# Four weight units of three narrow stages take x before its norm, and the norm's scale is put on their results

## The reference, cut to what matters

```python
h = x * rsqrt(mean(x * x) + eps) * gain + shift      # gain and shift: one number for each of 1024 channels
u = h @ w_in
```

## Time and profile before

| what | value |
|---|---|
| median of three runs | 2800.35 us (2799.84 to 2803.69) |
| the profiled execution, its own time | 2799.17 us |
| its span, first to last instruction | 2797.3 us |
| mean granted clock of TensorE | 0.994 of full speed |
| TensorE busy | 98% of the span |
| VectorE, ScalarE, GpSimd busy | 74%, 44%, 19% |

### The profile page before, as it was taken

One profiled execution on the slowest core, in us unless ns is written; L12 is line 12 of the kernel. 1 busy time (PEld: TensorE's weight loads), 2 busy tenths in 40 slices (PEclk: granted clock), 3 DMA queues, 4 the chain that ended last, 5 costly groups with the idle time before them and its releaser, 6 DMA issues.

```text
span 2797.3 us, 40204 instructions
## 1 busy us (share of the span) xinstructions
PE 2732.1 (98%) x15618; PEld 2320.2 (83%) x15618; DVE 2067.0 (74%) x3773; ACT 1216.9 (44%) x2228; POOL 522.2 (19%) x449
## 2 busy tenths in 40 slices
PE   7999999999999999999988999999999999999998
PEld 5888878668888878888885999889999888888887
DVE  6989895568989896564766766765896677777776
ACT  5323233453232342222445545565556444444444
POOL 1111114300111101010050000345898000000000
PEclk9999999999999999999999999999999999999999
DMA  7555533223555445354441566424654556655554
GB/s 290 194 186 192 185 136 112 76 103 123 202 182 190 175 154 189 122 191 145 146 148 45 191 216 216 146 84 151 197 152 121 185 190 192 192 193 190 190 190 132
DMA packets 123261, 462.50 MB, mean 165 GB/s; under 512 B 13504, under 2 KB 26688, under 8 KB 109888
## 3 DMA queue, kind: packets, MB, share of 16 engines
q1 hardware_dynamic: 109248, 359.27, 39.5%
q0 software_dynamic: 13824, 100.67, 9.3%
HBM read 452.93 MB, written 6.95 MB: 164 GB/s over the span
## 4 chain that ended last, share of the span: by engine, by line
PE 90%; DVE 7%; issue 1%; ACT 1%; DMA 1%; POOL 1%; POOLq 0%; DVEq 0%; ACTq 0%
PE bank L283 28%; PE bank L284 27%; PE bank L285 27%; PE bank L2469 2%; DVE weight_lo L182 1%; DVE extension_ffn L920 1%; DVE nmax L1397 1%; DMA extension_ffn<-in_w_mods 1%; DVE arena L544 1%; PE bank L940 1%; PE bank L941 1%; PE bank L385 0%; PE bank L508 0%; DVE extension_mixer L1390 0%; POOL weight_lo L235 0%
## 5 line engine op out<-in xcount | busy, mean ns | idle before, releaser
L175 ACT ACTIVATE weight_hi<-weight_ring 128x512 fp32r<-128x512 f32 x1272 | 798.7, 631 | 1188.2 <-PE bank L285 1187.1
L182 DVE TENSOR_TENSOR weight_lo<-weight_ring,weight_hi 128x512 fp32r<-128x512 f32 x1110 | 839.4, 760 | 430.6 <-ACT weight_hi L175 428.9
L283 PE MATMUL bank<-operand_hi,weight_hi 128*128 128x256 f32 (+1 forms) x3168 | 1045.4, 330 | 16.8 <-DVE operand_lo L561 5.6
L284 PE MATMUL bank<-operand_lo,weight_hi 128*128 128x256 f32 (+1 forms) x3168 | 1032.8, 326 | 0.0
L285 PE MATMUL bank<-operand_hi,weight_lo 128*128 128x256 f32 (+1 forms) x3168 | 1032.6, 326 | 0.0
L283 PEld LDWEIGHTS bank<-operand_hi,weight_hi 128*128 128x128 f32 x3168 | 602.2, 190 | 86.1 <-issue 16.1
L284 PEld LDWEIGHTS bank<-operand_lo,weight_hi 128*128 128x128 f32 x3168 | 602.6, 190 | 53.1 <-issue 0.5
L285 PEld LDWEIGHTS bank<-operand_hi,weight_lo 128*128 128x128 f32 x3168 | 602.1, 190 | 50.4
L920 DVE SCALAR_TENSOR_TENSOR extension_ffn<-extension_ffn,silu_c 128x512 f32<-128x512 f32 x532 | 388.4, 779 | 1.7
L235 POOL TENSOR_TENSOR weight_lo<-weight_ring,weight_hi 128x512 fp32r<-128x512 f32 x162 | 211.6, 1315 | 421.1 <-ACT weight_hi L175 418.3
L283 PE MATMUL bank<-hidden_hi_ffn,weight_hi 128*128 128x512 f32 (+1 forms) x704 | 256.6, 364 | 4.0 <-DVE arena L1173 4.0
(11 more groups left out here) (280 smaller groups left out, 2543.5 us busy)
## 6 DMA issues: line engine op xcount, KB each, us to landing
weight_ring<-in_ffn SPq DMA_DIRECT2D x272, 512.0 KB, 3.5
weight_ring<-in_experts SPq DMA_DIRECT2D x256, 512.0 KB, 3.5
extension_ffn<-in_w_mods POOLq DMA_DIRECT2D x96, 1024.0 KB, 7.6
weight_ring<-in_w_mix SPq DMA_DIRECT2D x56, 512.0 KB, 3.4
weight_ring<-in_w_second SPq DMA_DIRECT2D x52, 512.0 KB, 3.6
spill<-early_retrieve SPq DMA_DIRECT2D x45, 128.0 KB, 3.9
arena<-spill SPq DMA_DIRECT2D x45, 128.0 KB, 3.5
extension_mixer<-in_rel_bias SPq DMA_DIRECT2D x2, 1536.0 KB, 6.7
```

The source lines that it names most:

```text
L175: nc.scalar.activation(self.hi[:, g % 2, h], self.ring[:, g % NS, h], ACT.Copy).then_inc(self.rounded, 1)
L182: self.nc.vector.tensor_tensor(self.lo[:, g % 2, h], self.ring[:, g % NS, h], self.hi[:, g % 2, h].bitcast(F32), ALU.subtract).then_inc(se ...
L283: nc.tensor.matmul(out, a_hi, b_hi, start=start and n == 0, stop=False)
L284: nc.tensor.matmul(out, a_hi, b_lo, start=False, stop=False)
```

## The change

In three narrow entries (the mixer of the last layer, the network after it, and the second block) the first four weight units take x times gain, rounded and split in two parts as it stands before the norm (`raw`). Row by row the two words behind the 256 hold the shift, so that a result has 258 columns and column 256 is the weight's product with the shift. `round_raw` on ScalarE and `split_raw` on VectorE make this operand tile by tile, behind `square` and `gather` of the stage before; the rows of the operand buffers and of `hidden_hi` and `hidden_lo` become 528 words long for it. The first two units run as `late_pair`, which has `sums` behind tile 1 and `spread` behind tile 3, with no `keep_warm` in these entries. The results of the four units are multiplied by rs (a copy in SBUF) on VectorE and shifted on ScalarE; in the network the second of a pair is shifted in `hide`. Meanwhile scale, round and split make the ordinary operand for the fifth unit on, in the order of `late_scalar` and `late_vector`. In the mixer the context's 256 columns of the operand are made beside units 6 to 9, by `SplitNorm`.

Besides, everywhere in `AddProduct` and in the last part of every `Ffn`, ScalarE rounds the first half of a unit ahead of the square (and of `work.move`), and VectorE subtracts it ahead of `gather`. In the last layer's mixer the affine_selects wait for twelve evicted units instead of four. The eight `x2` of the second block move from beside units 2 to 5 to beside units 6 and 7. `Second` has `shifted` and `scaled` in the places of `evict` above; `shifted(3)` is followed by `turned_values`, four copies on ScalarE (lines 1967 and 1968). The core of the diff:

```diff
+def late_pair(units, pe, outs, norm):
+
+    nc = units.nc
+    for kt in range(KT):
+        i = kt // (KT // 2)
+        if kt % (KT // 2) == 0:
+            w = [units.half(pe, 0, j, i) for j in range(2)]
+        pe.wait_ge(norm.raw_in.sem, norm.raw_in.at(kt + 2))
+        b = slice(kt * P - i * HALF, (kt + 1) * P - i * HALF)
+        for j in range(2):
+            last = product(nc, outs[j], [((w[j][0][:, b], w[j][1][:, b]), norm.raw_operand(kt))], start=(kt == 0), stop=(kt == KT - 1))
+            if j == 0 and kt % (KT // 2) == KT // 2 - 1:
+                last.then_inc(units.used, 1)
+        if kt == 1:
+            norm.sums(pe)
+        if kt == 3:
+            norm.spread(pe)
+    last.then_inc(units.used, 2)
...
-        self.hi, self.lo = sb("operand_hi", [P, KT, width], F32R), sb("operand_lo", [P, KT, width], F32R)
+        pad = 16 if width > S else 0
+        hi, lo = (sb(f"operand_{part}", [P, KT, width + pad], F32R) for part in ("hi", "lo"))
+        self.hi, self.lo, self.raw = hi[:, :, 0:width], lo[:, :, 0:width], [part[:, :, width - S:width + 2] for part in (hi, lo) if pad]
...
+    def raw_operand(self, kt):
+        return self.raw[0][:, kt, :], self.raw[1][:, kt, :]
+
+    def round_raw(self, act, kt):
+
+        nc, hi = self.chip.nc, self.raw[0]
+        if kt == 0:
+            nc.scalar.activation(hi[:, :, S:S + 2], self.columns, ACT.Copy).then_inc(self.raw_rounded.sem, 1)
+        nc.scalar.activation(hi[:, kt, 0:S], self.x[:, kt, 0:S], ACT.Copy, scale=self.gain(kt, 0)).then_inc(self.raw_rounded.sem, 1)
+
+    def split_raw(self, dve, kt):
+
+        nc, (hi, lo) = self.chip.nc, self.raw
+        if kt == 0:
+            dve.wait_ge(self.raw_rounded.sem, self.raw_rounded.at(1))
+            nc.vector.tensor_tensor(lo[:, :, S:S + 2], self.columns, hi[:, :, S:S + 2].bitcast(F32), ALU.subtract)\
+                .then_inc(self.raw_in.sem, 1)
+        dve.wait_ge(self.raw_rounded.sem, self.raw_rounded.at(kt + 2))
+        nc.vector.scalar_tensor_tensor(lo[:, kt, 0:S], self.x[:, kt, 0:S], self.gain(kt, 0), hi[:, kt, 0:S].bitcast(F32),
+                                       ALU.mult, ALU.subtract).then_inc(self.raw_in.sem, 1)
...
+    def late_scalar(self, act, units, evict):
+
+        units.round(act, 0, 2, [0])
+        self.round_one(act, 0, 0)
+        self.round_one(act, 1, 0)
+        self.round_one(act, 2, 0)
+        units.round(act, 0, 2, [1])
+        units.round(act, 0, 3)
+        evict(0)
+        self.round_one(act, 3, 0)
+        units.round(act, 0, 4, [0])
+        evict(1)
+        self.round_one(act, 4, 0)
+        units.round(act, 0, 4, [1])
+        self.round_one(act, 5, 0)
+        self.round_one(act, 6, 0)
+        self.round_one(act, 7, 0)
+        units.round(act, 0, 5, [0])
+        evict(2)
+        units.round(act, 0, 5, [1])
+        evict(3)
...
+    def late_vector(self, dve, units, evict, middle=None):
+
+        units.subtract(dve, 0, 2, [0])
+        self.scale(dve, 0, 0)
+        self.scale(dve, 1, 0)
+        self.split(dve, 0, 0)
+        self.scale(dve, 2, 0)
+        self.split(dve, 1, 0)
+        units.subtract(dve, 0, 2, [1])
+        units.subtract(dve, 0, 3, [0])
+        self.copy_rstd(dve)
+        evict(0)
+        units.subtract(dve, 0, 3, [1])
+        self.scale(dve, 3, 0)
+        self.split(dve, 2, 0)
+        evict(1)
+        units.subtract(dve, 0, 4, [0])
+        self.scale(dve, 4, 0)
+        self.split(dve, 3, 0)
+        self.scale(dve, 5, 0)
+        self.split(dve, 4, 0)
+        units.subtract(dve, 0, 4, [1])
+        self.scale(dve, 6, 0)
+        self.split(dve, 5, 0)
+        self.scale(dve, 7, 0)
+        self.split(dve, 6, 0)
+        self.split(dve, 7, 0)
+        if middle:
+            middle()
+        units.subtract(dve, 0, 5, [0])
+        evict(2)
+        units.subtract(dve, 0, 5, [1])
+        evict(3)
...
+        if self.raw:
+            if kt == 1:
+                self.split_raw(dve, 0)
+            self.split_raw(dve, kt)
...
-                if not self.by_sums:
+                if not self.by_sums and not self.raw:
                     c.keep_warm(pe, self.spare, 3)
...
     def sums(self, pe):
-        self.chip.keep_warm(pe, self.spare, 5)
         self.sum(pe, KT - 1)
...
+            pe.wait_ge(self.norm.after.sem, self.norm.after.at(self.norm.first + 6))
+            late_pair(units, pe, [chip.bank[j][:, 0:S + 2] for j in range(2)], self.norm)
+            for u in range(2, self.late):
+                units.chunk(pe, 0, u, chip.bank[u][:, 0:S + 2], self.norm.raw_operand)
...
                 if half == 0 and n >= 2:
                     pe.wait_ge(self.gated.sem, self.gated.at(n - 1))
-                if u0 + u >= 2:
+                if u0 + u >= max(2, self.late):
                     units.chunk(pe, 0, u0 + u, chip.bank[2 * (u // 2 % 2) + half][:, 0:t],
-                                lambda kt: (self.hi[:, kt, 0:t], self.lo[:, kt, 0:t]))
+                                lambda kt: (self.hi[:, kt, 0:t], self.lo[:, kt, 0:t]),
+                                ready=self.norm.split_in if u0 + u == self.late else None)
...
+                if n0 + nh == FT:
+                    units.round(act, 0, u0 + 2 * nh + n + 2, [0])
+                    if n:
+                        self.then.square(act, n - 1)
+                    if work and n == KT - 1:
+                        work.move(act, work.n)
+                    units.round(act, 0, u0 + 2 * nh + n + 2, [1])
+                else:
+                    units.round(act, 0, u0 + 2 * nh + n + 2)
...
+        def hide(n):
+            g, hi, lo = self.gate_buf[:, n, 0:S], self.hid_hi[:, n, 0:S], self.hid_lo[:, n, 0:S]
+            dve.wait_ge(self.silu_done.sem, self.silu_done.at(n + 1))
+            dve.wait_ge(self.scaled.sem, self.scaled.at(2 * n + 2))
+            nc.vector.scalar_tensor_tensor(g, self.tb, chip.late_bias[:, 2 * n + 1:2 * n + 2], g, ALU.add, ALU.mult)\
+                .then_inc(self.ffn_step.sem, 1)
+            dve.wait_ge(self.ffn_step.sem, self.ffn_step.at(2 * n + 1))
+            first, rest = split_activations(nc, hi, lo, g)
+            first.then_inc(self.ffn_step.sem, 1)
+            dve.wait_ge(self.ffn_step.sem, self.ffn_step.at(2 * n + 2))
+            rest().then_inc(self.gated.sem, 1)
+
+        def evict(n):
+            dve.wait_ge(units.used, units.used_at(n))
+            nc.vector.tensor_copy(chip.late_bias[:, n:n + 1], chip.bank[n][:, S:S + 1])
+            nc.vector.tensor_tensor(self.tb if n % 2 else self.gate_buf[:, n // 2, 0:S], chip.bank[n][:, 0:S], chip.rs[:, :],
+                                    ALU.mult).then_inc(self.scaled.sem, 1)
+            if n == 3:
+                hide(1)
+
+        if self.late:
+            self.norm.split_raw(dve, KT - 1)
             self.norm.invert(dve)
-        self.norm.operands(dve)
+            self.norm.late_vector(dve, units, evict, lambda: hide(0))
...
             for n in range(KT):
+                units.subtract(dve, 0, u0 + 2 * nh + n + 2, [0])
                 if n0 + nh == FT and n >= 2:
                     self.then.gather(dve, n - 1)
-                units.subtract(dve, 0, u0 + 2 * nh + n + 2, [0])
...
-        pool.wait_ge(self.evicted.sem, self.evicted.at(4))
+        pool.wait_ge(self.evicted.sem, self.evicted.at(CH_K if self.last else 4))
...
+            if self.last and n < KT:
+                self.norm.round_one(act, 2 * n - KT, 1)
+                self.norm.round_one(act, 2 * n - KT + 1, 1)
...
+            if self.last and n < KT:
+                norm.scale(dve, 2 * n - KT, 1)
+                norm.scale(dve, 2 * n - KT + 1, 1)
+                norm.split(dve, 2 * n - KT, 1)
+                norm.split(dve, 2 * n - KT + 1, 1)
...
+            units.round(act, 0, n + 2, [0])
             if n:
                 self.then.square(act, n - 1)
-            units.round(act, 0, n + 2)
+            units.round(act, 0, n + 2, [1])
...
-        for j in range(6):
+        norm.late_vector(dve, units, scaled)
+        for j in range(4, 6):
             units.subtract(dve, 0, j + 2)
-            if j < 4:
-                norm.x2(dve, 2 * j)
-                norm.x2(dve, 2 * j + 1)
+            for kt in range(4 * (j - 4), 4 * (j - 3)):
+                norm.x2(dve, kt)
...
+                    ffn.then = norm1(chip, l, 1, T2, ffn.added, 2 * KT, kind=SplitNorm if last else Norm)
+                    if last:
+                        ffn.then.begin_raw(chip.raw, chip.mods[1][:, 3 * KT:4 * KT, :])
```

More of the change, by code:

```diff
@@ L1038, in __init__ @@
         self.then, self.double, self.transfers = None, False, []
+        self.late = 4 if norm.raw else 0
+        if self.late:
+            self.scaled, self.halves_out = chip.late_scaled.take(4), chip.late_out.take(2)
+            self.tb = chip.part(A_RSTD + 512, S)
         beside = {None: (0, 0, 0), 12: (0, 0, 1), 16: (2, 2, 1)}[work.n if work else None]
@@ L1198, in __init__ @@
         self.mix = None
```

(53 more changed lines are left out.)

146 lines of the change are left out of this document (109 added, 37 removed).

## The result

The changed kernel takes 2827.86 us (median; 2826.11 to 2830.94), the kernel before 2800.63 in the same comparison: a ratio of 1.0095, interval 1.0083 to 1.0108. It is 27 us slower; 2802.9 was forecast, with 2809 as the upper bound.

The account below looks back on a forecast made before the run. TensorE, busy 2732.1 of 2797.3 us, bounds the kernel, so only waits at three entries could give gains; 1.2 - 6.3 + 0.5 + 1.4 + 1.0 + 3.2 + 1.4 + 0.1 = +2.5, giving 2802.9 us, range 2790 to 2809.

Parts of the forecast that it names:

- 258 columns: Raw units of the entries: two more columns in 288 matmuls cost +0.1 us (0 to 0.3); 528-word rows cost nothing.
- The network ends of the first layer: Two first-layer networks: first half rounded and subtracted first makes transposes and sums about 0.6 later; +1.2 us (0 to 1.8).
- The last mixer: Last mixer's entry: shorter pair and moved affine_selects start unit 12 earlier, despite VectorE's queue; -6.3 us (-4.5 to -9).
- GpSimd later in the mixer: Last mixer: later convolution and pooling on GpSimd may slow VectorE at the attention's scaling; +0.5 us (0 to 1.5).
- The last network: Last network's entry: unit 4 waits for hidden tile 0 behind split 7, TensorE idles 5.4; +1.4 us (-3.5 to +2.5).
- the term of the clock: Last network's entry: the idle wait may bring a stretch at half clock; +1.0 us (0 to 1.7), nothing at other entries.
- The last eight units: Last network's last eight units: sums wait 0.54 for squares now behind rounds; six units, +3.2 us (0 to 5.5).
- The second block: Second block's entry: key copies and x2 delay the rotation, unit 8 starts later; +1.4 us (-4.6 to +3.8).
- rival C: All three entries are followed by half clock, 5.1 us in place of 1.0; 2807.0 us, slower, chance 0.15.
- Rival B: Gains at the entries stand; hidden tile 0, x2 and sums behind squares aren't waited for; 2787.6 us, faster, chance 0.20.

Follow-up runs that it names:

- p_rows528: Kernel before with only the rows of the operand buffers and hidden_hi and hidden_lo lengthened to 528 words: 2823.1 us, ratio 1.0077.
- a_views: Changed kernel with rows 512 words apart in all wide stages up to the last mixer, 528 from there on: 2803.69 us, ratio 1.0010.
- a_order: a_views with the old order: square ahead of both rounds, gather ahead of the subtraction: 2797.08 us, ratio 0.9987.
- a_hide: a_views with VectorE's `hide(0)` in the last network moved from behind split 7 to between split 3 and scale 5: 2799.21 us, ratio 0.9991.
- c_all_mended: Changed kernel with 512-word steps in wide stages, old square and gather order, earlier hidden tile 0, x2 behind the rotation's first step: 2795.76 us, ratio 0.9979.
- p_shift_operands: Kernel before with a 16-word spacer between weight_lo and operand_hi, rows still 512 words: 2806.59 us, ratio 1.0017.
- p_narrow64: Kernel before with operand and hidden rows starting 16 words further in, in the last layer's narrow stages, 512 apart: 2798.59 us, ratio 0.9991.

## Why the prediction was wrong

**The step that failed** is the sentence under "258 columns": "The 528-word rows change an address step only: nothing." It is +26 us in the wide stages by the pace (5424 products, 0.2316 in place of 0.2268) and 2 to 3 back in the narrow ones; p_rows528, which has that and nothing else, takes 22 us more than the kernel before. I had costed each instruction that the diff adds and moves, and taken for granted that the 5424 which it leaves alone keep their pace. No rival held it either: all of them were about waits and the clock. With the steps put back (a_views) the kernel takes 2803.69 us, 0.8 from the forecast of 2802.9, but that closeness is luck in part: misses of 1 to 3 us cancel in it, among them the 2 to 3 us that its 528-word rows give back in the narrow stages and the 1.7 us of the longer stretch of half clock in the second block, neither of which the forecast has. The terms, from the changed kernel's trace:

- *The network ends of the first layer*, +1.2 for two: from the last product to the transposes it is 0.78 in place of 0.32 at both, so +0.9. Right.
- *The last mixer*, -6.3: measured -7.1 to unit 12. Unit 2 starts 10.1 us behind the start of the last product, before 18.7, and the context chain takes 3.37 us a unit (3.43 worked out). Half of the gain is the affine_selects' place: 3.9, where the forecast names a wait of 3.2. Right.
- *GpSimd later in the mixer*, +0.5: from unit 12 to the last network the two traces differ by 0.4, about what the slower pace of the wide products there takes (96 x 0.0048). So nothing or near it. The attention's scaling, which reads a bank, took 0.41 us at 1503.32 beside a pooling step of GpSimd (1502.93 to 1504.00), 0.42 before; that is as the rule of the Trainium skill cited in the forecast has it. It wasn't tried by itself.
- *The last network*, +1.4 and +1.0 for the clock: measured 3.9 together. The wait was 5.56 (5.4 worked out) and begins and ends as described; the stretch of half clock behind it was 6.6 us or more, not 3.3, so the term of the clock was mis-sized: half of such a stretch is 3.3, which leaves 0.6 for the first term. The stretch is there in a_views and a_order, which keep the wait, and gone in a_hide and c_all_mended, which shorten it.
- *The last eight units*, +3.2: 0.66 in place of 0.12 from the product ahead to each of six sums, 0.54 each. Right; and a_order shows it. The mark moves by 1.2 only, since the products of 256 columns between take 0.1183 for 0.120.
- *The second block*, +1.4: 34.62 against 33.43 from the last of the eight units to unit 8, +1.2. Right.
- *258 columns*, +0.1: in the mixer raw products one behind another take 0.1204 from start to start, 0.0021 more than the 0.1183 of the narrow ones behind it, so +0.6 for 288.
- *Nothing was put down* for what lies behind unit 8 of the second block: +1.6, the longer stretch of half clock there.

The low clock did not come at the first or the third entry, as forecast; rival C fails there. Rival B, that the gains at the entries stand, holds for the mixer alone.

## What to carry to other kernels

A change of a buffer's layout is a change to every instruction that reads it: before the moved instructions are costed, count those that keep their place and get another address. Compare two traces first in a window where the bounding engine never waits; if the count of its instructions differs there, no story of waits explains the loss. And an entry that is shortened on TensorE gains only what VectorE's queue behind it lets through.

## What the runs showed of the hardware

What I had not expected: how fast TensorE takes these fp32r matmuls one behind another depends on where the moving operand's row starts against the weights' row. For 512 columns p_shift_operands and a_views show it together; for 256 columns p_narrow64 shows that the operands' place counts.

| rows of the moving operand against those of the weights | 512 columns | 256 columns |
|---|---|---|
| same place modulo 256 bytes (steps of 2048; 2304 in operand_hi) | 0.2268 | 0.1200 |
| all 64 bytes off | 0.2294 | 0.1178 |
| steps of 2112 bytes | 0.2316 | 0.1183 |
| steps of 2176 bytes | 0.2320 | 0.1189 |

These are mean microseconds from start to start. The two widths go opposite ways, which I can't explain: whether it is a meeting of the weight load with the moving reads or something else wasn't tried. Other offsets than 64 bytes alone weren't either, and the period of four tiles at steps of 2176 bytes doesn't fit a rule of 256 bytes. The 0.2268 to 0.2320 are the products of operand and hidden tiles from 100 to 330 us, those of 256 columns lie in the last network.
